# Expert sweep of a decoder block: the scatter-add into the output in whole rows of 4 KB in one chain, with six whole product tiles

## The chip, the cores and the metric

The kernel runs on the 8 cores of one Trainium2 chip. Each core has its own sequence of the batch (4096 tokens of 1024 values) and its own copy of all weights; the cores do not exchange data. The time is that of the slowest core in microseconds (us). A core has TensorE (PE: matmuls and transposes), VectorE (DVE), ScalarE (ACT), GpSimd (POOL: here it issues the indirect DMAs and writes their descriptors) and SyncE (SP: here it issues the weight loads), and 16 DMA engines that all queues share.

## The reference, cut to what matters

```python
h2 = modulate(rmsnorm(x, norm2_gain[l]), shift2, scale2)          # x: after the token mixer
# hierarchical_moe: top-1 group of 4, top-2 of its 4 experts; combine (T, 4, 4) has two nonzeros per token
for gi in range(N_EXPERT_GROUPS):
    a = jnp.einsum('td,edf->tef', hf, w_gate[gi])
    b = jnp.einsum('td,edf->tef', hf, w_up[gi])
    hid = jax.nn.silu(a) * b * combine[:, gi, :, None]
    out = out + jnp.einsum('tef,efd->td', hid, w_down[gi])
x = x + gate2[:, None, :] * y_moe
```

So each token goes through two of 16 experts, and two products of 1024 float32 values are added to its row of `x`.

## The kernel before

The first three quarters of the time are the token mixer, the router and the conversion of the expert weights to bfloat16 in DRAM (`w_bf`). They leave `x` in `out` (4096 rows of 4 KB and 128 spare rows) and the normalised tokens with their 16 weights in `h2d` (rows of 2112 bytes). The change touches only what follows, the function `moe` at the end: the sweep.

The sweep first computes on VectorE which token stands in which row of which block: 79 blocks of 128 rows, all rows of a block for one expert (`idx`, one column of 128 row numbers for each block; `idxh`, the same for rows of half the length). Then it goes through the blocks p = 0 to 78. Two lanes alternate: even p take blocks 0, 1, 2, ..., odd p take blocks 40, 41, .... Each lane has its own half of the six weight slots (`wts[p % 2]`), so an expert's weights stay while its blocks follow one another in the lane, and when the expert changes six chunks of 512 KB come anew. All instructions are in program order on each engine; the order of a step is in the loop at the end of `moe`:

- `gather(p + 6)`: POOL issues an indirect DMA that brings 128 rows of `h2d` into one of 7 buffers.
- `x_t(p + 2)`: PE transposes the block, ACT copies it out, DVE picks the weight of each row.
- `g_mm(p + 1)`, `u_mm(p + 1)`: 8 matmuls each for gate and up; ACT takes SiLU, DVE forms gate x up x weight.
- `d_t(p)`, `d_mm(p)`: PE transposes the hidden block and multiplies it with the down weights into PSUM banks 4 and 5, one bank for each half of the 1024 output columns.
- `scatter(b, 0)`, `scatter(b, 1)`, called in `d_mm`: DVE multiplies a bank by `g2b` (the gate) into a tile of 128 x 512 float32; POOL issues an indirect DMA that adds the 128 rows of 2 KB to the output (`compute_op=ALU.add`).
- `w_load(p + 2, (4, 5))`, `w_load(p + 3, (0, 1, 2, 3))`: SP issues the weight chunks; where the expert stays, the address lies out of bounds and the DMA moves nothing.

A token can stand in two blocks, and an add reads a row, adds and writes it. So adds to the same bytes must not be in flight together. The kernel sees to it with one region for each half of the columns, `r_outh[0]` and `r_outh[1]`: POOL waits before each add until the last add to the same half has landed. There are thus two chains, and an add of the left half and one of the right half may be in flight together. While POOL waits, all that stands behind in its order waits too, the gathers among it.

The product tiles are a ring of 11 halves (`yp`): six in the three `f32a` tiles, five in `BB`. DVE waits before it overwrites a tile until that tile's add has landed.

The trace names all operations that the helper `K.op` records as L166; the gathers are L1272, the adds L1358, the weight loads L1287. The product tiles show up as `f32a<-PS,g2b` and `BB<-PS,g2b`, the adds as `out<-f32a,BB` and `out<-BB`, the weight chunks as `slot<-w_bf`.

Of the kernel before, what the change touches and what calls it, by code (L numbers as in the profile page):

```python
# [6 lines left out]
F32 = mybir.dt.float32  # L7
BF16 = mybir.dt.bfloat16
F16 = mybir.dt.float16
I32 = mybir.dt.int32  # L10
U8 = mybir.dt.uint8
AF = mybir.ActivationFunctionType
ALU = mybir.AluOpType
# [8 lines left out]
NB = 79  # L22
# [196 lines left out]
def build_nc(n_st=4, dbg=False, upto=None):  # L219
# [36 lines left out]
    out = nc.dram_tensor("out", [T + 128, D], F32, kind="ExternalOutput").ap()  # L256
# [6 lines left out]
    K = Sync()  # L263
    es = ExitStack()

    def sb(name, shape, dt):
        return es.enter_context(nc.sbuf_tensor(name, list(shape), dt))
# [13 lines left out]
    g2b = sb("g2b", [128, 1024], BF16)  # L281
# [32 lines left out]
    f32a = RR([sb(f"f32a{i}", [128, 1024], F32) for i in range(3)], "f32a")  # L314
# [21 lines left out]
    bank_r = [Region(f"bank{i}") for i in range(8)]  # L336
# [17 lines left out]
    def bank(i, w=512, off=0):  # L354
        return PS[:, i * 512 + off: i * 512 + off + w]
# [101 lines left out]
    for g in range(8):  # L457
# [17 lines left out]
         reads=[r_c0], writes=[r_c])  # L475
    K.op("act", lambda e: e.activation(out=esink[:], in_=esink[:], func=AF.Exp), reads=[r_const], writes=[r_const])
    K.op("dve", lambda e: e.tensor_tensor(out=WmT[:], in0=wsf[:].rearrange("p (g t) -> p g t", g=8),
                                          in1=mkt[:, 0:128].unsqueeze(1).to_broadcast([128, 8, 128]), op=ALU.mult),
         reads=[wsf_r, mkt_r], writes=[r_const])
# [13 lines left out]
    for hh in range(2):  # L493
        K.op("pe", lambda e, hh=hh: e.matmul(PS[0:1, (b0 + hh) * 512:(b0 + hh + 1) * 512], ones_bf[:, 0:1],
                                            WmT[:, 4 * hh:4 * hh + 4, :], start=True, stop=True),
             reads=[r_const], writes=[br_[hh]])
    K.op("act", lambda e: e.activation(out=r2r[0:1, :], in_=PS[0:1, b0 * 512:(b0 + 2) * 512], func=AF.Copy),
         reads=br_, writes=[r2r_r])
    b0, br_ = nb(2)
    for g in range(8):  # L500
        K.op("pe", lambda e, g=g: e.matmul(PS[:, b0 * 512 + g * 128: b0 * 512 + (g + 1) * 128], r2l[0:2, g, :],
                                          r2r[0:2, g * 128:(g + 1) * 128], start=True, stop=True),
             reads=[r_const, r2l_r, r2r_r], writes=[br_[g // 4]], inc=(g % 4 == 3))
# [20 lines left out]
    def ada_rows(units, dst, dst_r):  # L524
        for n_, u in enumerate(units):
# [13 lines left out]
         reads=[r_const, r_mod], writes=[r_const])  # L539
# [607 lines left out]
    def moe():  # L1147
        olds = [r_B1, r_B2] + r_acc
        r_lh = r_lhs[0]
        BBf = BB[:]  # L1150
        BH = BBf[:, 0:64 * NB].bitcast(F16).rearrange("p (a b) -> p a b", a=64)
        r_bh = K.alias("bh", olds)
        o_ = 64 * NB
# [6 lines left out]
        idx = BBf[:, o_:o_ + 2 * 80].bitcast(I32)  # L1160
        tab = BBf[:, o_ + 160:o_ + 320].bitcast(I32)
        r_idx = K.alias("idx", olds)
        r_tab = K.alias("tab", olds)
        o_ += 320
        o_ += (-o_) % 16
        ys = [f32a.tiles[i][:, 512 * h:512 * (h + 1)] for i in range(3) for h in range(2)]
        ys_r = [K.alias(f"y{i}{h}", [f32a.regs[i]]) for i in range(3) for h in range(2)]
        for i in range(5):
            ys.append(BBf[:, o_ + 1024 * i:o_ + 1024 * (i + 1)].bitcast(F32))
            ys_r.append(K.alias(f"y{i}b", olds))  # L1170
        yp = RR(ys, "y")
        idxh = [BBf[:, 16064 + 160 * h:16224 + 160 * h].bitcast(I32) for h in range(2)]
        outh = out.rearrange("t (h c) -> (t h) c", h=2)
        r_outh = [K.alias(f"out{h}", [r_out]) for h in range(2)]
        NXG = 7
        hTf = hT[:].rearrange("p k t -> p (k t)")
        xgs = [hTf[:, 1056 * i:1056 * (i + 1)] for i in range(NXG)]
# [4 lines left out]
        def bid(p):  # L1182
            return p // 2 if p % 2 == 0 else LANE + p // 2
# [13 lines left out]
        W = [r_wk]  # L1197

        def wop(fn, reads=(), writes=None):
# [3 lines left out]
                                      in1=row[:, 148:179].unsqueeze(1).to_broadcast([128, 16, 31]), op=ALU.is_gt), reads=ptr_)  # L1203
# [7 lines left out]
        for sh in (1, 2, 4, 8):  # L1211
# [8 lines left out]
             reads=W + [r_oh], writes=[tmp_r])  # L1220
# [4 lines left out]
        for s_ in range(4):  # L1225
            K.op("dve", lambda e: e.tensor_tensor(
                out=BH[:, 16 * s_:16 * s_ + 16, :], in0=bk[:, 16 * s_:16 * s_ + 16].unsqueeze(2).to_broadcast([128, 16, NB]),
                in1=iob.unsqueeze(1).to_broadcast([128, 16, NB]), op=ALU.is_equal), reads=W + [r_const], writes=[r_bh])
            K.op("dve", lambda e: e.tensor_tensor(
                out=BH[:, 16 * s_:16 * s_ + 16, :].rearrange("p (k b) n -> p k b n", k=2),  # L1230
                in0=BH[:, 16 * s_:16 * s_ + 16, :].rearrange("p (k b) n -> p k b n", k=2),
                in1=col[:, 8 * s_:8 * s_ + 8].unsqueeze(1).unsqueeze(3).to_broadcast([128, 2, 8, NB]), op=ALU.mult),
                 reads=[r_bh, r_const], writes=[r_bh])
        pi, pir = nb(1)
        for a in range(64):
            K.op("pe", lambda e, a=a: e.matmul(bank(pi, NB), LH[:, a, :], BH[:, a, :], start=(a == 0), stop=(a == 63)),
                 reads=[r_lh, r_bh], writes=pir, inc=(a == 63))
        va = wk[:, 592:592 + NB]
# [3 lines left out]
        wop(lambda e: e.tensor_scalar(out=vb, in0=bank(pi, NB), scalar1=0.0, scalar2=col[:, 32:33], op0=ALU.is_equal, op1=ALU.mult), reads=pir)  # L1242
        wop(lambda e: e.scalar_tensor_tensor(out=va, in0=va, scalar=2048.0, in1=vb, op0=ALU.add, op1=ALU.add))
        K.op("dve", lambda e: e.tensor_copy(out=idx[:, 0:NB], in_=va), reads=W, writes=[r_idx])
        for h in range(2):
            K.op("dve", lambda e: e.tensor_scalar(out=idxh[h][:, 0:NB], in0=va, scalar1=2.0, scalar2=float(h), op0=ALU.mult, op1=ALU.add),
                 reads=W, writes=[r_idx])

        K.op("dve", lambda e: e.tensor_tensor(out=ehot, in0=iob.unsqueeze(2).to_broadcast([128, NB, 16]),
                                              in1=cumb.unsqueeze(1).to_broadcast([128, NB, 16]), op=ALU.is_ge),  # L1250
             reads=W + [r_const], writes=[r_eh])
# [4 lines left out]
                                              in1=eb.unsqueeze(2).to_broadcast([128, NB, 16]), op=ALU.is_equal),  # L1256
             reads=W + [r_const], writes=[r_eh])
# [85 lines left out]
        def d_mm(p, ht, ht_r):  # L1343
            for fl in range(4):
                for dh in range(2):
                    c_ = 4 + fl // 2
                    K.op("pe", lambda e, fl=fl, dh=dh, c_=c_: e.matmul(
                        bank(4 + dh), ht[:, fl * 128:(fl + 1) * 128],
                        wts[p % 2][c_][:, (fl % 2) * 1024 + dh * 512:(fl % 2) * 1024 + (dh + 1) * 512], start=(fl == 0), stop=(fl == 3)),
                         reads=[ht_r, wts_r[p % 2][c_]], writes=bank_r[4 + dh:5 + dh], inc=(dh == 1 and fl % 2 == 1) or fl == 3)  # L1350
            b = bid(p)
            for dh in range(2):
                scatter(b, dh, *yp.next())

        def scatter(b, dh, y, y_r):
            K.op("dve", lambda e: e.tensor_tensor(out=y, in0=bank(4 + dh), in1=g2b[:, 512 * dh:512 * (dh + 1)], op=ALU.mult),
                 reads=bank_r[4 + dh:5 + dh] + [r_g2], writes=[y_r])
            K.dma_call("pool", lambda e: e.indirect_dma_start(  # L1358
                out=outh, out_offset=bass.IndirectOffsetOnAxis(ap=idxh[dh][:, b:b + 1], axis=0),
                in_=y, in_offset=None, compute_op=ALU.add),  # L1360
                       reads=[r_idx, y_r], writes=[r_outh[dh]])

        ys_r[0:6] = [K.alias(f"y{i}{h}", [f32a.regs[i]]) for i in range(3) for h in range(2)]
        yp.regs = ys_r
        AHEAD = NXG - 1
        for p in range(AHEAD):
# [8 lines left out]
        for p in range(NB):  # L1375
            if p + AHEAD < NB:
                gather(p + AHEAD)
            if p + 2 < NB:
                x_t(p + 2)
            if p + 1 < NB:  # L1380
                sl = g_mm(p + 1)
            ht = d_t(p, *hd)
            if p + 1 < NB:
                hd = u_mm(p + 1, *sl)
            d_mm(p, *ht)
            if p + 2 < NB:
                w_load(p + 2, (4, 5))
            if p + 3 < NB:
                w_load(p + 3, (0, 1, 2, 3))

    try:
        for st_ in range(n_st):
            body(st_)
        conv_step(len(conv))
        moe()
    except _Stop:
        pass
# [88 lines left out]
```

How the kernel before makes its waits and increments, by code:

```python
            def body(eng):  # L156
                for item in self.prog[e]:
                    if item[0] == "wait":
                        eng.wait_ge(sems[item[1]], item[2])
                    elif item[0] == "call":
                        ins = item[1](eng)
                        if item[2] is not None:
                            ins.then_inc(sems[item[2]], item[3])
                    else:
                        name, a, k = item[1]
                        ins = getattr(eng, name)(*a, **k)
                        if item[2] is not None:
                            ins.then_inc(sems[item[2]], item[3])
```

## Time and profile before

| | us |
|---|---|
| median of 3 runs | 2673.39 (2668.78 to 2675.87) |
| the profiled execution | 2670.27 |
| its span on the slowest core (core 0) | 2668.6 |
| spans of the other cores | 2640.1 to 2662.5 |

The whole page has PE busy for 1933.4 us, DVE for 1105.5, ACT for 870.2 and POOL for 670.0; these are sums over stages with different limits. The sweep's blocks run from about 2065 us to the end at 2668.6. In the trace, the first product of the sweep is formed at 2081 us and the last at 2642 us.

How to read the views: times are in us from the first instruction. A row of the timeline has the start, the duration, the engine, the line, the operation and `out<-in`, and in brackets how long the engine had been idle before and what ended that. The DMA view gives for a stretch the packets and bytes of each queue and the share of the time of all 16 DMA engines that its packets took; q0 is POOL's queue (gathers and adds), q1 is SP's (weights, and before the sweep the plain loads and stores). From a share, the length of the stretch and 16 engines follows the engine time of a packet.

### The profile page before, as it was taken

The numbers are of one execution on the slowest core, as the hardware profiler recorded it, in microseconds if no ns is written. First come the engines' busy times: TensorE is split into PE (matmuls) and PEld (weight loads), VectorE is DVE, ScalarE is ACT, GpSimd is POOL, SyncE is SP. The second block draws the span as 40 slices with busy tenths as digits, with TensorE's granted clock in tenths as the row PEclk, the third lists the DMA queues.
The fourth block names the chain that finished last, engine by engine and source line by source line (L and its number), as shares of the span: only waits on it lengthen the run. The fifth ranks groups of instructions, "written<-read, shape, count | busy, mean of one in ns | idle before, by whom it ended". The sixth has DMA issues, their size and how long they took to land.

```text
span 2668.6 us, 37330 instructions; the slowest of 8 cores (2640.1 to 2668.6 us)
## 1 busy us (share of the span) xinstructions
PE 1933.4 (72%) x10857; PEld 986.8 (37%) x11023; DVE 1105.5 (41%) x2174; ACT 870.2 (33%) x1356; POOL 670.0 (25%) x658
## 2 busy tenths in 40 slices
PE   1557619966675798667579866758982889888895
PEld 1223314434333344423334442334452444444442
DVE  1354512345445425544543554453356223332332
ACT  0416511134155324315531441553130222222231
POOL 1200520011103301110430111042010455555564
PEclk9989559987896699789679978967995988899998
DMA  7763898864306946420693442062132898999987
GB/s 122 165 120 71 96 111 157 146 214 159 67 32 75 117 129 186 167 56 32 82 130 121 141 160 56 32 80 95 64 119 73 231 207 170 191 184 214 188 163 142
DMA packets 124569, 337.87 MB, mean 127 GB/s; under 512 B 26762, under 2 KB 56850, under 8 KB 114132
## 3 DMA queue, kind: packets, MB, share of 16 engines
q0 software_dynamic: 79264, 200.26, 45.1%
q1 hardware_dynamic: 45108, 135.21, 14.4%
q8 instruction: 95, 1.56, 0.3%
q14 instruction: 102, 0.84, 0.1%
HBM read 526.89 MB, written 136.32 MB: 249 GB/s over the span
## 4 chain that ended last, share of the span: by engine, by line
PE 50%; DVE 15%; DMA 14%; issue 9%; ACT 8%; POOL 2%; SPq 1%; DVEq 1%; ACTq 0%; POOLq 0%; another core or an unknown queue 0%
PE PS L166 50%; DMA slot<-w_bf 6%; ACT FH L166 4%; DVE PT L166 4%; DVE small L166 3%; DVE BB L166 3%; DVE f32a L166 2%; DMA slot<-w_ada 2%; ACT bfh L166 2%; DMA triu<-k_tri 1%; DVE hT L166 1%; DMA slot<-w_out 1%; POOL small L166 1%; ACT f32a L166 1%; DMA out<-f32a,BB 1%
## 5 line engine op out<-in xcount | busy, mean ns | idle before, releaser
L166 PE MATMUL PS<-hT,slot 128*128 128x512 bf16 x2256 | 535.0, 382 | 12.2 <-DMA slot<-w_in 8.1
L166 PE MATMUL PS<-slot,B 128*128 128x512 bf16 x1701 | 445.5, 404 | 94.1 <-DMA slot<-w_bf 70.9
L166 PEld LDWEIGHTS PS<-hT,slot 128*128 128x128 bf16 x2304 | 226.0, 99 | 272.5 <-issue 22.0
L166 PEld LDWEIGHTS PS<-slot,B 128*128 128x128 bf16 x1776 | 171.6, 103 | 292.1 <-issue 148.9
L166 ACT ACTIVATE bfh<-PS 128x512 bf16<-128x512 f32 (+2 forms) x431 | 233.4, 595 | 72.0 <-PE PS L166 70.7
L166 POOL TENSOR_TENSOR PT<-bfh,etab 128x512 bf16<-128x512 bf16 (+1 forms) x128 | 147.6, 1164 | 429.8 <-ACT bfh L166 310.4
L166 POOL TENSOR_TENSOR small<-small 128x1 f32<-128x1 f32 x96 | 78.2, 815 | 696.6 <-DVE small L166 696.6
L166 PE MATMUL PS<-BB,slot 128*128 128x512 bf16 x997 | 244.2, 385 | 1.9 <-issue 0.7
L166 ACT ACTIVATE FH<-PS,cst 128x512 f32<-128x512 f32 x128 | 88.0, 687 | 338.4 <-PE PS L166 338.3
L166 DVE SCALAR_TENSOR_TENSOR bfh<-PS,small,FH 128x512 bf16<-128x512 f32 x79 | 59.3, 751 | 320.6 <-PE PS L166 307.0
L166 ACT ACTIVATE B<-PS 128x1024 bf16<-128x1024 bf16 x79 | 80.9, 1024 | 333.0 <-PE PS L166 333.0
L166 PE MATMUL PS<-slot,hT 128*128 128x512 bf16 (+1 forms) x756 | 179.0, 402 | 2.2 <-issue 1.9
L166 DVE TENSOR_TENSOR PT<-bfh,etab 128x512 bf16<-128x512 bf16 (+1 forms) x128 | 130.6, 1020 | 113.4 <-ACT bfh L166 113.4
L1358 POOL DMA_INDIRECT out<-f32a,BB x88 | 137.5, 1563 | 138.9 <-DMA out<-f32a,BB 46.0
L166 ACT ACTIVATE FH<-PS 128x512 f32<-128x512 f32 x175 | 104.5, 597 | 170.8 <-PE PS L166 164.7
L166 PE MATMUL PS<-slot,bfh 128*128 128x512 bf16 x631 | 157.4, 394 | 1.2 <-DVE f32a L166 1.1
L166 PEld LDWEIGHTS PS<-BB,slot 128*128 128x128 bf16 x1024 | 101.4, 99 | 123.8 <-issue 6.4
L1358 POOL DMA_INDIRECT out<-BB x70 | 109.3, 1562 | 111.8 <-DMA out<-BB 41.8
L166 ACT ACTIVATE BB<-PS 128x512 bf16<-128x512 f32 (+1 forms) x96 | 71.0, 739 | 201.3 <-PE PS L166 200.7
L166 DVE TENSOR_TENSOR B<-PS,FH 128x512 bf16<-128x512 f32 x64 | 44.3, 691 | 188.8 <-ACT FH L166 188.8
L166 PE MATMUL PS<-vaug,PT 128*128 128x65 bf16 x1008 | 83.9, 235 | 52.3 <-DVE ytm L166 27.1
L166 PEld LDWEIGHTS PS<-slot,hT 128*128 128x128 bf16 x768 | 86.5, 114 | 87.1 <-issue 44.6
(157 smaller groups left out, 2276.5 us busy)
## 6 DMA issues: line engine op xcount, KB each, us to landing
slot<-w_bf SPq DMA_DIRECT2D x474, 512.0 KB
w_bf<-w_ch POOLq DMA_DIRECT2D x96, 512.0 KB
FH<-x SPq DMA_DIRECT2D x32, 512.0 KB
BB<-x SPq DMA_DIRECT2D x32, 512.0 KB
out<-BB SPq DMA_DIRECT2D x32, 512.0 KB
slot<-w_ada POOLq DMA_DIRECT2D x12, 1024.0 KB
slot<-w_in POOLq DMA_DIRECT2D x10, 1024.0 KB
h2d<-PT SPq DMA_DIRECT2D x32, 256.0 KB
```

What stands on the lines that cost most here:

```text
L166: ins = getattr(eng, name)(*a, **k)
L1358: K.dma_call("pool", lambda e: e.indirect_dma_start(out=outh, out_offset=bass.IndirectOffsetOnAxis(ap=idxh[dh][:, b:b + 1], axis=0), in_=y ...
```

## The change

Each block's product is now one tile of 128 x 1024 float32. DVE still fills it with two multiplies of 512 columns, and one indirect DMA adds its 128 rows of 4 KB to the output. The row numbers are those of `idx`, so the two operations that formed `idxh` are gone. There is one region for the output (`r_out`), so POOL waits before each add until the add before it has landed. The ring of product tiles has six whole tiles: the three `f32a` tiles and three in `BB`.

```diff
-        ys = [f32a.tiles[i][:, 512 * h:512 * (h + 1)] for i in range(3) for h in range(2)]
-        ys_r = [K.alias(f"y{i}{h}", [f32a.regs[i]]) for i in range(3) for h in range(2)]
-        for i in range(5):
-            ys.append(BBf[:, o_ + 1024 * i:o_ + 1024 * (i + 1)].bitcast(F32))
-            ys_r.append(K.alias(f"y{i}b", olds))
+        ys = [t[:] for t in f32a.tiles] + [BBf[:, o_ + 2048 * i:o_ + 2048 * (i + 1)].bitcast(F32) for i in range(3)]
+        ys_r = [K.alias(f"yb{i}", olds) for i in range(6)]
         yp = RR(ys, "y")
-        idxh = [BBf[:, 16064 + 160 * h:16224 + 160 * h].bitcast(I32) for h in range(2)]
-        outh = out.rearrange("t (h c) -> (t h) c", h=2)
-        r_outh = [K.alias(f"out{h}", [r_out]) for h in range(2)]
...
-        for h in range(2):
-            K.op("dve", lambda e: e.tensor_scalar(out=idxh[h][:, 0:NB], in0=va, scalar1=2.0, scalar2=float(h), op0=ALU.mult, op1=ALU.add),
-                 reads=W, writes=[r_idx])
...
             b = bid(p)
+            y, y_r = yp.next()
             for dh in range(2):
-                scatter(b, dh, *yp.next())
-
-        def scatter(b, dh, y, y_r):
-            K.op("dve", lambda e: e.tensor_tensor(out=y, in0=bank(4 + dh), in1=g2b[:, 512 * dh:512 * (dh + 1)], op=ALU.mult),
-                 reads=bank_r[4 + dh:5 + dh] + [r_g2], writes=[y_r])
+                K.op("dve", lambda e: e.tensor_tensor(out=y[:, 512 * dh:512 * (dh + 1)], in0=bank(4 + dh),
+                                                      in1=g2b[:, 512 * dh:512 * (dh + 1)], op=ALU.mult),
+                     reads=bank_r[4 + dh:5 + dh] + [r_g2], writes=[y_r])
             K.dma_call("pool", lambda e: e.indirect_dma_start(
-                out=outh, out_offset=bass.IndirectOffsetOnAxis(ap=idxh[dh][:, b:b + 1], axis=0),
+                out=out[:, :], out_offset=bass.IndirectOffsetOnAxis(ap=idx[:, b:b + 1], axis=0),
                 in_=y, in_offset=None, compute_op=ALU.add),
-                       reads=[r_idx, y_r], writes=[r_outh[dh]])
-
-        ys_r[0:6] = [K.alias(f"y{i}{h}", [f32a.regs[i]]) for i in range(3) for h in range(2)]
+                       reads=[r_idx, y_r], writes=[r_out])
+
+        ys_r[0:3] = f32a.regs
         yp.regs = ys_r
```

How the instructions stand on POOL near the end of the sweep, before: gathers (`hT<-h2d`) and adds (`out<-`), with the semaphores that POOL waits for ahead of each (`dve` is the product, `dpl` and a number an earlier DMA of POOL's queue).

```order
L1358 DMA out<-BB 8448x512 [waits dve,dpl6]
L1272 DMA hT<-h2d,BB 128x528 [waits pe]
L1358 DMA out<-BB 8448x512 [waits dpl11,dve,dpl8]
L1358 DMA out<-BB 8448x512 [waits dve,dpl9]
L1272 DMA hT<-h2d,BB 128x528 [waits pe]
L1358 DMA out<-f32a,BB 8448x512 [waits dpl14,dve,dpl11]
L1358 DMA out<-f32a,BB 8448x512 [waits dve,dpl12]
L1272 DMA hT<-h2d,BB 128x528 [waits pe]
```

The same stretch of POOL's order in the changed kernel.

```order
L1263 DMA hT<-h2d,BB 128x528 [waits dpl9,pe]
L1348 DMA out<-BB 4224x1024 [waits dve,dpl6]
L1263 DMA hT<-h2d,BB 128x528 [waits dpl11,pe]
L1348 DMA out<-BB 4224x1024 [waits dve,dpl8]
L1263 DMA hT<-h2d,BB 128x528 [waits dpl13,pe]
L1348 DMA out<-f32a,BB 4224x1024 [waits dve,dpl10]
```

Between two gathers there was a pair of adds, each with a wait for the add two before it; now there is one add, with a wait for the one just before it.

On VectorE, one step near the end of the sweep, before: the two multiplies that write the product are `BB<-PS,g2b`.

```order
L166 SCALAR_TENSOR_TENSOR bfh<-PS,small,FH 128x512 [waits pe,act]
L166 TENSOR_TENSOR BB<-PS,g2b 128x512 [waits pe,dpl8]
L166 TENSOR_TENSOR BB<-PS,g2b 128x512 [waits pe,dpl10]
L166 TENSOR_TENSOR bfh<-hT,BB 128x16 [waits dpl15]
L166 TENSOR_REDUCE small<-bfh 128x1 [waits dve]
```

And one step there in the changed kernel.

```order
L166 SCALAR_TENSOR_TENSOR bfh<-PS,small,FH 128x512 [waits pe,act]
L166 TENSOR_TENSOR BB<-PS,g2b 128x512 [waits pe,dpl2]
L166 TENSOR_TENSOR BB<-PS,g2b 128x512 [waits pe,dve]
L166 TENSOR_TENSOR bfh<-hT,BB 128x16 [waits dpl7]
L166 TENSOR_REDUCE small<-bfh 128x1 [waits dve]
```

The order is the same; the first multiply now waits for the add that frees the whole tile, and the second waits for the first.

## Rows read from the trace of the kernel before

**Rows 1.** Busy time of each engine, stretches inside the sweep and at its end.
```profile
core 0: us, PE busy (x) PEld busy (x) DVE busy (x) ACT busy (x) POOL busy (x), PEclk, DMA share, GB/s
2200.00:2300.00 100.00, 89.87 (x492) 43.46 (x500) 32.07 (x70) 28.46 (x40) 53.36 (x39) 0.89 0.86 168
2400.00:2500.00 100.00, 84.04 (x465) 40.83 (x473) 29.91 (x66) 27.43 (x39) 54.51 (x41) 0.91 0.94 201
2600.00:2668.00 68.00, 36.47 (x206) 17.70 (x208) 15.15 (x31) 12.01 (x18) 34.33 (x24) 0.84 0.75 143
```

**Rows 2.** Who waited for whom from 2000 us: total, times, longest.
```profile
PE PS L166 <- DMA slot<-w_bf: 70.9, 53, 4.3
```

**Rows 3.** Timeline of DVE: two steps whose weights are there.
```profile
2309.42 1.29 DVE L166 TENSOR_TENSOR BB<-PS,g2b 128x512 f32<-128x512 f32 x2 [0.76 <-PE PS L166]
...
2315.27 1.29 DVE L166 TENSOR_TENSOR BB<-PS,g2b 128x512 f32<-128x512 f32 x2 [0.76 <-PE PS L166]
```

**Rows 4.** All adds (L1358), and the idle time of POOL before them.
```profile
L1358 POOL DMA_INDIRECT out<-f32a,BB x88: 1550/1554/1640, 2082.9 to 2661.5; - x88
L1358 POOL DMA_INDIRECT out<-BB x70: 1550/1554/1579, 2104.7 to 2650.7; - x70
its engine sat idle before it (us, times) until:
  DMA out<-f32a,BB: 64.6, 26
  PE PS L166: 59.8, 50
  DMA out<-BB: 58.4, 24
  DVE small L166: 22.6, 8
  DVE bfh L166: 20.4, 13
  issue: 18.0, 32
  DVE BB L166: 4.1, 3
  DVE f32a L166: 3.0, 2
```

**Rows 5.** Timeline of DVE and POOL, the last product and the adds behind it.
```profile
2642.42 1.29 DVE L166 TENSOR_TENSOR f32a<-PS,g2b 128x512 f32<-128x512 f32 x2 [1.93 <-PE PS L166]
...
2653.82 1.55 POOL L1358 DMA_INDIRECT out<-f32a,BB  x1 [1.58 <-issue]
2656.27 1.55 POOL L1358 DMA_INDIRECT out<-f32a,BB  x1 [0.90 <-DMA out<-BB]
2659.21 1.55 POOL L1358 DMA_INDIRECT out<-f32a,BB  x1 [1.39 <-DMA out<-f32a,BB]
2661.45 1.55 POOL L1358 DMA_INDIRECT out<-f32a,BB  x1 [0.70 <-DMA out<-f32a,BB]
```

**Rows 6.** Chain that ended last: start, duration; one add from issue to landing.
```profile
2653.82 4.63 DMA out<-f32a,BB
```

**Rows 7.** DMA view, 2640 to 2660 us: only adds in flight.
```profile
q0 software_dynamic: 994, 1.83, 68.9%
```

**Rows 8.** DMA view, 1958.9 to 1962.8 us: one plain store, 128 rows of 2 KB.
```profile
DMA packets 145, 0.28 MB, mean 71 GB/s; under 512 B 16, under 2 KB 16, under 8 KB 144
...
q1 hardware_dynamic: 144, 0.26, 17.9%
```

**Rows 9.** DMA view, 1962.8 to 1966.8 us: one plain store, 128 rows of 4 KB.
```profile
q1 hardware_dynamic: 144, 0.52, 32.2%
```

**Rows 10.** DMA view, 2252 to 2277.4 us: weights, adds and gathers together.
```profile
q1 hardware_dynamic: 1452, 5.26, 61.7%
q0 software_dynamic: 897, 1.91, 37.9%
```

**Rows 11.** DMA view, 2065 to 2669 us: the whole sweep.
```profile
q0 software_dynamic: 28969, 62.42, 64.3%
q1 hardware_dynamic: 13824, 50.34, 23.8%
```

**Rows 12.** Groups by form, 2040 to 2064 us: the two `idxh` operations are among these.
```profile
L166 DVE TENSOR_SCALAR BB<-BB 128x79 int32<-128x79 f32 x2 | 0.4, 201 | 0.2
```

## The prediction

> **What bounds the kernel now.** I read the stretches of the busy-time view first. Inside the sweep [rows 1] PE is busy for 84 to 90% and the DMA engines for 86 to 94% of the time; in the last 68 us PE falls to 54%. POOL is near 54% and DVE near 32% and bound nothing by their work. So two resources are close to full, and the question is which wait ends last. Where the weights of a step are there, PE sets the pace: the same DVE multiply comes every 2315.27 - 2309.42 = 5.85 us [rows 3]. From the first add (2082.9, [rows 4]) to the last product (2642.42, [rows 5]) there are 78 such steps in 559.5 us; at 5.85 us they would take 456 us. The other 103 us are stalls, and the list of waits names them: PE waits for the weight chunks, 70.9 us in 53 direct waits [rows 2]. So in the body of the sweep PE and, where an expert changes, the landing of 3 MB of weights are the bound.
>
> At the end it is another one. After the last product, eight adds are still to be issued or to land, and the kernel ends 26 us later (2668.6 against 2642.4 [rows 5]). The adds lag there by some four blocks, so the two chains of adds are not far from being a bound over the whole sweep. POOL's idle time ahead of the adds says the same [rows 4]: 123.0 us in 50 of 158 adds ended with the landing of an earlier add (64.6 + 58.4), and 109.9 us with PE or DVE, that is, with the product (59.8 + 22.6 + 20.4 + 4.1 + 3.0). Less some 13 us before the first add, 97 us are slack of the adds.
>
> **What one add costs now.** In the tail an add to one half starts at 2653.82 and the next to the same half at 2659.21, a pitch of 5.39 us [rows 5]. 4.63 of them are issue to landing [rows 6], the rest is POOL's reaction, 0.76. Of the 4.63, POOL writes descriptors for 1.55 [rows 4]. How long do the packets hold the DMA engines? Where only adds move, 994 packets take 68.9% of 20 us of 16 engines [rows 7]: 0.222 us each. A transfer of 128 rows is 144 packets, 128 rows and 16 small ones (under 512 B) [rows 8]; so an add holds each engine for 9 x 0.222 = 2.00 us. The other 3.4 us of the pitch are fixed.
>
> **What one add of 4 KB rows costs.** The trace has no add with such rows. It has plain stores with both: 2 KB rows take 0.179 x 3.9 x 16 = 11.2 us of engine time [rows 8], 4 KB rows 0.322 x 4.0 x 16 = 20.6 us [rows 9]. So 2 KB more in each row cost (20.6 - 11.2) / 16 = 0.59 us an engine for one stream, with nothing fixed of note. A 2 KB plain store holds an engine for 0.70 us and a 2 KB add for 2.00, nearly three times as long: an add has to fetch the product, fetch the old row, and write.
> - Lower bound: the two fetches overlap and only one stream is paid, +0.59. Pitch 5.98 us.
> - Upper bound: everything doubles, 4.00 us instead of 2.00. Pitch 7.39 us.
> - I take two streams one after the other, +1.18, with what is left of an add packet (0.222 less 2 x 0.074) as a fixed part that longer rows don't pay twice. Each engine is then held for 3.18 us, and the pitch is 6.57 us. It stands between the ends, a little nearer the lower; [rows 10] lean the same way: with weights alternating, q0's packets take 0.379 x 25.4 x 16 / 897 = 0.172 us, less than when adds run alone, so part of the 0.222 is waiting and not bytes.
>
> The descriptor writing stays at 1.55 us, 128 rows as before.
>
> **The change, part by part.**
> - *One chain instead of two.* Before, both halves shared the fixed 3.4 us of a pitch; now one add must do the whole block, and a block needs 6.57 us of chain instead of 5.39: 1.18 x 79 = +93 us of chain over the sweep. That is above PE's 5.85, so with weights present the adds now fall behind by 0.7 us a block, and catch up only while PE waits for weights. The slack of 97 us can absorb it where it lies next to a backlog. I count three quarters of it as usable (PE's stalls come in bunches, and a chain that has caught up starves): 73 us. The net is 93 - 73 = +20 us. Where the backlog reaches six tiles, DVE's first multiply waits for a free tile; behind it in DVE's order stand the next block's row weights and gate product, and PE's next `d_mm` waits for the banks 4 and 5. That is how a late add gets to PE.
> - *Less DMA time.* The adds of a block hold each engine for 3.18 instead of 4.00 us, 0.82 x 79 = 65 us of the 604 in [rows 11]. Where weights land, q0 has 37.9% and q1 61.7% of the engines [rows 10]; with adds a fifth cheaper q0 would fall to some 32 to 33% and the weights gain 8%. On 103 us of stalls that is -8 us.
> - *Ring of tiles.* 12 halves instead of 11, no term. A tile is now held until its whole row has landed, which is in the pitch.
> - *POOL.* 79 adds fewer at 1.55 us. POOL is half idle, and the gathers are six steps ahead: nothing. The gathers stand behind a waiting add; they need 1.02 us of an interval in which POOL waits anyhow.
> - *DVE.* The two operations for `idxh`, 0.2 us each [rows 12], stood ahead of the first gather: -0.5 us with their gaps. The add now starts after the second multiply: +0.6 on the first add. Together 0.
>
> Sum: 20 - 8 = +12 us. The profiled execution took 2670.3, so 2682; the median of the runs is 3.1 us above it, hence **2685**.
>
> A check from the other side, the chain alone, never starved: first add at 2083.6, then 78 pitches of 6.57 (512 us), and where weights move each of the 8 packets of an add lets one weight packet of 0.173 us [rows 10] go first, 1.4 us an add. Weights hold the engines for 0.238 x 604 = 144 us [rows 11], at 61.7% that is 233 us of the time or 29 adds: 40 us. The last add needs 7.15 + 1.18 from issue to the end. Sum 2644: this is a floor, some 38 us under my sum, and those are the starvation that the first sum has as unusable slack.
>
> The Trainium skill (DMA: Bandwidth & Descriptors, Anatomy of one DMA) gives about 2.0 us fixed and bytes / 436e9 for a DMA of POOL's queue, and advises to coalesce. By that, 256 KB more would be an estimated 0.6 us, the lower bound above, and the change would win. The trace does not agree for adds of today: by the rule the bytes of one are 0.6 us, the engines are held for 2.00. The same page (Queues, rings and completion order) says that a DMA engine goes round its queues packet by packet; that bears on the fourth rival.
>
> **Rivals.**
> 1. *Faster: only one stream is paid.* For it: the 0.172 us under mixed load, and that plain packets pay only bytes. Against it: add packets take three times as long as plain ones. Pitch 5.98: +47 us, all within the slack. The adds hold an engine for 2.59 instead of 4.00 us a block, weights gain 14% of 103 us, -15, and the four blocks of lag at the end shrink by two, -8. Together -23: 2650.
> 2. *Slower: an add's time goes with its bytes, or the row is moved as two 2 KB packets after all*, so that the change doesn't do what it says on the DMA engines. For it: the adding unit may be what takes the time, and nothing in the trace speaks of its rate. Pitch 7.39: +158 us, 73 absorbed, +85; the chain alone gives 2083.6 + 78 x 7.39 + 40 + 9 = 2709, +40. Between them +62: 2735. It decides from a pitch of about 7.1 us on, the mean of PE's steps with its stalls (559.5 / 78 = 7.17).
> 3. *Slower: the weights.* An add packet keeps its turn for 3.18 / 9 = 0.35 us instead of 0.22 before a weight packet gets one. While a backlog keeps q0 full, weights get 0.173 / (0.173 + 0.353) = 33% instead of 44% of an engine. Against it: one chain leaves 3.4 us free in each pitch, in which the weights have the engines alone. If it wins, the -8 turns into +19: 2712.
>
> **How the numbers follow.** Forecast 0.40, range of its own 2665 to 2705; rival 1 0.33; rival 2 0.17; rival 3 0.10. A run of this kernel can be told from no change from 0.3% on, that is 8 us: below 2665.4 is faster, above 2681.4 slower. Faster: 0.30 of rival 1 and 0.02 of the forecast, 0.32. Same: 0.03 and 0.12, 0.15. Slower: 0.26 of the forecast and rivals 2 and 3, 0.53. For the range I leave out the lower part of rival 1 and what lies above rival 2's middle, about a tenth each: 2648 to 2740.
>
> **What the profile after would show.** 144 packets for each add, so some 17,700 in q0 over the sweep (79 x (144 + 80 for a gather)) instead of 28,969, with the same bytes; twice as many per add would be rival 2's second half. A pitch of adds in the tail of 6.57 (5.98: rival 1; 7.39: rival 2). POOL's idle time before adds ended mostly by `out`, hardly by PE or DVE. More than 26 us from the last product to the end, up to six adds of 6.6 us. If DVE waits for an add (`out`) at all, the backlog filled the ring. PE's wait for weights: 65 us if the relief is right, above 80 if rival 3 is. I am wrong if the adds are no longer late at the end, or if PE's stalls, not the adds, carry the difference.

## The result: 2.7% slower

| | before | after |
|---|---|---|
| median | 2674.63 us (4 runs, 2668.78 to 2677.97) | 2746.85 us (4 runs, 2742.71 to 2885.77) |
| profiled execution | 2670.27 us | 2748.19 us |
| its span, slowest core | 2668.6 us (core 0) | 2746.6 us (core 2) |

The ratio is 1.0267, with a 95% interval of 1.0241 to 1.0294. (It, the ratios below and times given for single runs leave out executions in which the four cores of one die ran at a visibly lower TensorE clock; the highest time of after is one; the medians are over all runs.) Predicted were 2685 and "slower": the sign was right, the size was not, since +72 us stand against +12. The part before the sweep is the same in both kernels, but its length differs between executions: the first gather on core 0 starts between 2047 and 2067 us in the traces of this case, at 2060.6 in that of before and 2067.2 in that of after. That difference between the two profiled executions is no effect of the change.

The list of waits of the changed kernel, core 2, from 2000 us: who waited for whom, total, times, longest. It answers to [rows 2].

```profile
POOL out L1348 <- PE PS L166: 190.6, 38, 14.5
POOL out L1348 <- DMA out<-f32a,BB: 115.4, 19, 9.0
PE PS L166 <- DMA hT<-h2d,BB: 112.0, 43, 7.9
POOL out L1348 <- DMA out<-BB: 109.9, 18, 10.4
...
PE PS L166 <- DMA slot<-w_bf: 21.6, 17, 3.7
```

PE's wait for weights is down from 70.9 to 21.6 us, and in its place stands a wait that was hardly there: 112.0 us for the gathered rows `hT<-h2d`. That looks like a problem with the gathers. The rows of the adds say otherwise. First all 79 of them (against [rows 4]), then the end of the timeline (against [rows 5]).

```profile
L1348 POOL DMA_INDIRECT out<-f32a,BB x40: 1549/1586/1640, 2093.2 to 2737.5; - x40
L1348 POOL DMA_INDIRECT out<-BB x39: 1549/1586/1604, 2120.5 to 2731.0; - x39
...
DMA to landing us min/median/max: 5.7/6.7/12.5
```

```profile
2711.99 1.49 DVE L166 TENSOR_TENSOR f32a<-PS,g2b 128x512 f32<-128x512 f32 x2 [1.78 <-PE PS L166]
2717.52 1.56 POOL L1348 DMA_INDIRECT out<-BB  x1 [5.09 <-DMA out<-f32a,BB]
2724.22 1.55 POOL L1348 DMA_INDIRECT out<-BB  x1 [5.13 <-DMA out<-BB]
2731.01 1.55 POOL L1348 DMA_INDIRECT out<-BB  x1 [5.25 <-DMA out<-BB]
2737.47 1.55 POOL L1348 DMA_INDIRECT out<-f32a,BB  x1 [4.90 <-DMA out<-BB]
```

A pitch is the time from the start of one add to the start of the next in its chain. In the tail it is (2737.47 - 2717.52) / 3 = 6.65 us. Over the whole sweep it is (2737.5 - 2093.2) / 78 = 8.26 us. PE's own pace was 5.85 a block [rows 3], and 7.17 with its stalls for weights. So the chain is slower than PE all the way.

The chain that ended last, about 2500 us: start, duration, what.

```profile
2514.15 9.39 DMA out<-f32a,BB
2523.58 0.54 issue
2524.33 9.85 DMA out<-f32a,BB
2534.22 0.54 issue
2534.97 7.88 DMA out<-BB
2542.90 0.54 issue
2543.65 5.99 DMA out<-BB
2549.68 0.54 issue
2550.43 6.34 DMA out<-BB
```

Each add starts 0.8 us after the one before has landed, and nothing else stands between. That holds for the whole sweep: on this core 75 of the 78 adds behind the first start within 0.9 us of that landing, and the other three within 2.1. The list of waits above seems to say something else, since it puts 190.6 us of POOL's waits down to PE. An add waits for its product and for the add before it, and the list can name only one of the two. The next two rows are such a case, an add from issue to landing and the add behind it.

```profile
2460.15 6.47 DMA out<-f32a,BB
```

```profile
2467.41 1.59 POOL L1348 DMA_INDIRECT out<-f32a,BB  x1 [4.37 <-PE PS L166]
```

The first lands at 2466.62 and the second starts at 2467.41, 0.8 us later like all the others, though PE is named. So a wait that the list puts down to PE or DVE may well be one for the chain.

From issue to landing an add takes about 6 us, but 8 to 10 in the stretch from 2514 to 2543. What moves when an add is slow: first the DMA view of the tail (2717.5 to 2724.2 us, one add alone), then of 2439 to 2449.3 us, in which the add issued at 2436.69 and a gather behind it are on their way and weights land.

```profile
q0 software_dynamic: 144, 0.52, 48.7%
```

```profile
q1 hardware_dynamic: 552, 2.02, 60.5%
q0 software_dynamic: 215, 0.78, 40.0%
```

Alone, the add is 144 packets (no splitting of the 4 KB rows) and holds an engine for 0.487 x 6.7 = 3.26 us; the prediction had 3.18. Beside weights, 552 weight packets pass while q0 moves 215 (of the 224 of this add and its gather), 2.6 for one, and this add takes 12.55 us to land.

### The profile page after: what moved, and what is told of

Same layout as the page of the kernel before. It is cut to its first block, busy times and chain, and to the rows that moved or that the text cites. A ratio compares the mean times of both kernels' runs of the same rounds, so it can differ in the third digit from the quotient of the medians.

```text
span 2746.6 us, 37261 instructions; the slowest of 8 cores (2717.4 to 2746.6 us)
## 1 busy us (share of the span) xinstructions
PE 1948.7 (71%) x11023; PEld 989.4 (36%) x11023; DVE 1119.3 (41%) x2172; ACT 870.2 (32%) x1356; POOL 546.6 (20%) x579
## 4 chain that ended last, share of the span: by engine, by line
PE 40%; DMA 24%; DVE 15%; issue 9%; ACT 8%; POOL 2%; DVEq 1%; SPq 0%; ACTq 0%; POOLq 0%; another core or an unknown queue 0%
PE PS L166 40%; DMA out<-BB 8%; DMA out<-f32a,BB 6%; ACT FH L166 4%; DVE PT L166 4%; DVE small L166 3%; DVE BB L166 3%; DMA slot<-w_bf 2%; DVE f32a L166 2%; ACT bfh L166 2%; DMA slot<-w_ada 2%; DMA hT<-h2d,BB 2%; DMA triu<-k_tri 1%; DVE hT L166 1%; DMA slot<-w_out 1%
## 5 line engine op out<-in xcount | busy, mean ns | idle before, releaser
L166 PE MATMUL PS<-hT,slot 128*128 128x512 bf16 x2304 | 543.0, 384 | 10.4 <-DMA slot<-w_in 9.8
L166 PE MATMUL PS<-slot,B 128*128 128x512 bf16 x1776 | 457.0, 407 | 38.2 <-DMA slot<-w_bf 21.6
L166 PEld LDWEIGHTS PS<-slot,B 128*128 128x128 bf16 x1776 | 177.1, 105 | 236.3 <-issue 92.7
L166 ACT ACTIVATE B<-PS 128x1024 bf16<-128x1024 bf16 x79 | 80.9, 1024 | 407.6 <-PE PS L166 407.6
L166 PE MATMUL PS<-ident_b,hT 128*128 128x128 bf16 x632 | 53.9, 235 | 113.3 <-DMA hT<-h2d,BB 112.0
L166 PE MATMUL PS<-WmT,BB 128*128 128x128 bf16 x256 | 30.1, 301 | 116.7 <-DVE BB L166 116.7
```

The lines of the kernel that those rows point to most:

```text
L166: ins = getattr(eng, name)(*a, **k)
```

## The experiments

Two theories for the first round. A: the one chain of adds is the bound, the late gathers are how it reaches PE. B: the gathers are the bound, because they stand behind waiting adds in POOL's order. A third, C, says that the bytes and packets of the adds matter, by what they do to the weights.

**whole_lead10.** More buffers for the gathers, so that they are issued 10 steps ahead (four buffers lie in the part of `BB` that is free by then).

```diff
-        NXG = 7
+        NXG = 11
-        xgs = [hTf[:, 1056 * i:1056 * (i + 1)] for i in range(NXG)]
+        xgs = [hTf[:, 1056 * i:1056 * (i + 1)] for i in range(7)] + [BBf[:, 1056 * i:1056 * (i + 1)] for i in range(NXG - 7)]
-        r_xg = [K.alias(f"xg{i}", [r_lh]) for i in range(NXG)]
+        r_xg = [K.alias(f"xg{i}", [r_lh] if i < 7 else [r_bh]) for i in range(NXG)]
```

> The changed kernel with 11 gather buffers instead of 7, so that a gather is issued 10 steps ahead instead of 6. Theory A (the chain of adds is the bound): in the changed kernel one add follows the other almost without a gap, 78 pitches of 8.26 us in the mean; PE's 112 us of waits for gathers are only the way in which the late chain holds it. Then nothing is gained: 2747 within 10 us, the waits for gathers fall below 30 us and as much appears as DVE waiting for a free product tile. Theory B (the gathers are the bound: they stand behind waiting adds in POOL's order): PE's waits for gathers go and take their time with them, 2747 less 60 to 100, so 2650 to 2690.

Measured: 2748.39 us, ratio to before 1.0252 (1.0219 to 1.0285). Nothing is gained. The waits of its slowest core, 3:

```profile
DVE BB L166 <- DMA out<-BB: 138.2, 25, 12.6
DVE f32a L166 <- DMA out<-f32a,BB: 134.8, 26, 10.8
```

PE's wait for gathers is down to 9.9 us, and DVE now waits 273 us for a free product tile instead. Theory B is out: take away one place where the backlog is held, and it is held at the next one.

**whole_two_lanes.** Whole rows, but one chain for the even and one for the odd steps. Padding rows of both lanes went to the same spare rows; the odd lane gets 128 spare rows of its own in `out` and `h2d`.

```diff
+        r_outl = [K.alias(f"out{i}", [r_out]) for i in range(2)]
...
-                       reads=[r_idx, y_r], writes=[r_out])
+                       reads=[r_idx, y_r], writes=[r_outl[p % 2]])
...
+        vc = wk[:, 928:928 + NB - LANE]
+        wop(lambda e: e.tensor_scalar(out=vc, in0=bank(pi, NB)[:, LANE:NB], scalar1=0.0, scalar2=128.0, op0=ALU.is_equal, op1=ALU.mult), reads=pir)
...
+        wop(lambda e: e.tensor_tensor(out=va[:, LANE:NB], in0=va[:, LANE:NB], in1=vc, op=ALU.add))
```

> The changed kernel with whole rows of 4 KB, but two chains: POOL waits before an add for the last add of the same lane (even or odd steps), not for the one before. The padding rows of the odd lane go to spare rows of their own; the result is the reference's as long as the two lanes don't reach rows of the same token in neighbouring steps, which holds for this routing. Theory A: the chain was the bound, two whole-row adds in flight hide the 3.4 us fixed part; 2640 to 2675, PE hardly waits for gathers, fewer than three blocks of lag at the end. Theory B says the same for another reason. Theory C (the bytes: 4 KB adds hold the DMA engines and slow the weights, or each other): no more than a third of the 72 us comes back, 2720 or above.

Measured: 2694.2 and 2691.7 us. About 55 of the 72 us come back. The list of waits has no add any more that waits for an add, and on cores 4 to 7 each add for which the last landing of its lane is known (30 to 41 of 77 a core) starts 2 us or more after that landing. So the single chain was the main cause, and theory C's "no more than a third" is out. But the time stays 13 us above the kernel before as timed beside it (2680), and above the 2675 that theory A allowed.

**whole_no_weights, half_no_weights.** Every lane keeps its first expert's weights; the same edit in the changed kernel and in the one before.

```diff
+        wop(lambda e: e.memset(fr, 16.0 * CHB))
+        wop(lambda e: e.memset(fr[:, LANE:LANE + 1], 0.0))
         wop(lambda e: e.tensor_tensor(out=fr, in0=fr, in1=eb, op=ALU.add))
```

> The changed kernel in which each lane keeps the first expert's weights it loaded, so that no weights move during the sweep (the products are those of the wrong experts). Theory A with the pitch of 7.1 to 7.3 us that the trace shows between weight loads: first add near 2092, 78 x 7.2 = 562, 8 for the last: 2662, PE still waits for gathers or tiles, since 7.2 is above its 5.85. Of the 85 us gained all is the time that weight packets add to the chain. If PE were the bound instead: 2092 + 456 + 10 = 2560.

> The kernel before (halves, two chains), with no weights moving during the sweep in the same way. Two chains need 5.4 to 5.7 us a block, below PE's 5.85: PE's pace decides, 2081 + 78 x 5.85 + 10 = 2550, some 110 us less than the changed kernel without weights. If halves were held back by the chains too, 2600 or more.

Measured: medians of 2661.87 us and 2574.91 us, ratios to before 0.9948 (0.9896 to 1.0000) and 0.9603 (0.9567 to 0.9639). The first meets its forecast. The second is 25 us above it. All adds of whole_no_weights, core 6, and of half_no_weights, core 1:

```profile
L1350 POOL DMA_INDIRECT out<-f32a,BB x40: 1550/1587/1640, 2091.2 to 2645.2; - x40
```

```profile
L1360 POOL DMA_INDIRECT out<-f32a,BB x88: 1549/1553/1639, 2091.5 to 2564.8; - x88
```

In half_no_weights a block takes (2564.8 - 2091.5) / 78 = 6.07 us of adds, not the 5.4 to 5.7 that were expected. That is above PE's 5.85: the adds fall behind, the last product stands at 2545.53, and the kernel ends 27 us after it instead of 10. The rest of the 25 us is a later start (2091.5 instead of 2081).

In whole_no_weights the pitch is (2645.2 - 2091.2) / 78 = 7.10 us. So the weights add 8.26 - 7.10 = 1.16 us to a pitch, 90 us over the sweep, and PE waits for gathers even without them (70.0 us).

**whole_no_weights_no_gathers.** As whole_no_weights, and the gathers stop after the seventh (`if p >= 7: return` at the head of `gather`).

> whole_no_weights with no gathers after the seventh either, so that in the steps only the adds use the DMA engines and POOL (the blocks then repeat the first seven). Theory A: the one chain is the bound with the pitch of the tail, 6.65 us, at every step: 2091 + 78 x 6.65 + 8 = 2618, 37 to 44 us less than whole_no_weights (2656 to 2663, pitch 7.10); those 0.45 us a step are then what the gathers add to an add. If the difference between tail and body is something else (the other cores' traffic, the late tiles), the time stays at 2650 or above.

Measured: 2667.73 and 2658.11 us. The expectation of theory A failed: the time stays. Core 0, all adds and POOL's idle time before them:

```profile
L1352 POOL DMA_INDIRECT out<-f32a,BB x40: 1552/1557/1640, 2073.2 to 2623.7; - x40
...
  DMA out<-BB: 197.4, 36
  DMA out<-f32a,BB: 187.6, 34
```

(2623.7 - 2073.2) / 78 = 7.06 us, with nothing but adds in the core's queues. So the gathers cost the chain nothing, and 7.06 is its pitch undisturbed by its own core. Why the tail of the changed kernel is 0.4 us shorter stays open. That other cores are done by then doesn't look like the reason: the last two adds are 6.4 to 6.8 us apart on each of the eight cores of after, also on the one with the shortest span (core 5, 2717.4 us against 2746.6).

**half_one_chain.** The kernel before, rows of 2 KB, one chain.

```diff
-        r_outh = [K.alias(f"out{h}", [r_out]) for h in range(2)]
+        r_outh = [K.alias("out", [r_out])] * 2
```

> The kernel before with its rows of 2 KB and its 11 tiles, but one chain for both halves, so that never two adds are in flight. Theory A: each block needs two pitches of 5.39 us in the tail, 10.8, and more under load by the same factor as whole rows (8.26 to 6.65, 1.24), 13.4: 2085 + 78 x 12 to 13.4 = 3020 to 3130. So going from two chains to one costs some 400 us, and whole rows give about 300 of them back. If the number of chains mattered little and the row size a lot: below 2800.

Measured: ratio 1.1497 (1.1473 to 1.1520), 3072.08 and 3074.99 us, as theory A expected. Going to one chain alone costs 400 us; whole rows give some 325 of them back. The 72 us of the change are the difference of these two large parts. Core 3:

```profile
L1358 POOL DMA_INDIRECT out<-f32a,BB x88: 1549/1552/1639, 2075.8 to 3051.7; - x88
```

Its 158 adds have a pitch of (3051.7 - 2075.8) / 157 = 6.2 us.

**whole_store.** The changed kernel with `compute_op=ALU.add` left out.

> The changed kernel with the same one chain of whole rows, but each DMA writes its rows instead of adding them (the output then lacks x and one of the two products). A plain store of 4 KB rows holds an engine for 1.29 us instead of 3.26. Theory A: issue to landing falls from 5.9 to some 4 us, the pitch to 4.8 us, below PE's 5.85; the chain is no bound any more and weights get more of the engines: 2610 to 2645. If the chain's fixed part under weight traffic (POOL's descriptors, the landing) were what counts and not the add's own work, 2700 or more would stay.

Measured: 2633.61 us, ratio 0.9830 (0.9792 to 0.9867), within theory A's range. Core 5:

```profile
L1348 POOL DMA_INDIRECT out<-f32a,BB x40: 961/984/1005, 2090.5 to 2623.4; - x40
...
DMA to landing us min/median/max: 3.3/3.5/10.1
```

The same chain with a landing of 3.5 us instead of 6.7 (medians) is no bound. So it is what an add takes beyond a store that makes one chain too slow: of the 3.2 us, 0.6 are POOL's descriptors (984 against 1586 ns), the rest lies behind them, in the read, add and write.

**half_four_lanes.** Before, with a chain for each half and lane: in `scatter` the region is `r_outh[dh + 2 * (p % 2)]`, and the spare rows are as in whole_two_lanes.

> The kernel before (rows of 2 KB), with four chains instead of two: POOL waits before an add for the last add of the same half and the same lane. Padding rows of the odd lane go to spare rows of their own, as in whole_two_lanes, so the two differ in the size of the rows alone. Theory A (chains bound the adds): no add waits for an add any more, the 26 us from the last product to the end shrink to some 12, and PE's stalls for weights stay near 70 us: 2655 to 2668, faster than both kernels. Theory C (with the chains out of the way the adds crowd the weights): PE's waits for weights rise above 80 us, as they did in whole_two_lanes (87), and the time is 2675 to 2695. Against whole_two_lanes: equal if rows of 4 KB cost the weights nothing extra; 20 to 30 us less if they do.

Measured: 2673.92 us, ratio 1.0000 (0.9988 to 1.0013). The list of waits has no add that waits for another (on core 6 the landing before is known for all 154 adds that have one in their chain, and none starts less than 3.7 us after it), and the slowest core ends 12 us after its last product:

```profile
2664.27 1.29 DVE L166 TENSOR_TENSOR f32a<-PS,g2b 128x512 f32<-128x512 f32 x2 [1.93 <-PE PS L166]
...
2668.82 1.55 POOL L1363 DMA_INDIRECT out<-f32a,BB  x1 [0.30 <-issue]
```

Half of the lag at the end is gone as expected, and nothing is won: PE's wait for weights, 63.4 us before in the mean of the eight cores, is 73.5 here. The time lies between the two theories' ranges (up to 2668 and from 2675) and so do the waits (near 70 and above 80). What was gained at the end was lost to the weights: adds that aren't held back take DMA engines that the weights need, as theory C has it, though by less than it said.

**whole_two_lanes_lead10.** whole_two_lanes and the buffers of whole_lead10 together.

> whole_two_lanes (rows of 4 KB, one chain for each lane) with 11 gather buffers, gathers issued 10 steps ahead. In whole_two_lanes PE waits 9 to 11 us for gathers, nearly all at the start, and 70 to 87 us for weights. If the weights are the bound there: no change, 2690 to 2700. If late gathers hid behind another name: 10 us or more faster.

Measured: 2687.39 us, ratio 1.0054 (1.0039 to 1.0069). whole_two_lanes was 13 us over before and this is 14 over it as timed beside each, so late gathers hid nothing there. Whole rows stay 0.5%, some 14 us, slower than half_four_lanes, which has the same lanes. Slowest core, 5:

```profile
PE PS L166 <- DMA slot<-w_bf: 90.7, 52, 5.4
```

In the mean of the cores PE waits 79.5 us for weights, against 73.5 with rows of 2 KB. The rest of the 14 us I can't place.

**half_tail_lanes.** If two chains serve the weights and cost only at the end, four chains belong at the end alone.

```diff
+            if p >= 68 and not r_outt:
+                r_outt.extend(K.alias(f"outt{h}", [r_outh[h % 2]]) for h in range(4))
+            r_o = r_outt[dh + 2 * (p % 2)] if p >= 68 else r_outh[dh]
...
-                       reads=[r_idx, y_r], writes=[r_outh[dh]])
+                       reads=[r_idx, y_r], writes=[r_o])
```

> The kernel before with its two chains up to step 67 and four chains (half and lane, as in half_four_lanes) from step 68 on, where few weights or none are left to load. The lag of the adds at the end (26 us from the last product to the end) should shrink to some 13 us, as it did in half_four_lanes, while the adds don't crowd the weights before. Theory A/C together (two chains throttle the adds to the weights' good, and cost only at the end): 10 to 14 us less than before, ratio 0.995 to 0.996. If the lag of the end is made good anyway, or the last weights still move then: within 3 us of before.

Measured: 2670.14 us, ratio 0.9974 (0.9951 to 0.9996). It is the fastest of the versions that compute the whole result, some 7 us ahead of before, where 10 to 14 were expected; core 3 ends 12 us after its last product. Like all versions with lanes it rests on the routing: both experts of a token are in one group, the lanes meet in a group only around block 40, and the even lane comes there at its end, the odd lane at its start. With nearly all tokens in one group it would not hold.

## Why the prediction was right and wrong

- *The price of one add: right.* Of the three prices of a 4 KB row, the one taken, two streams after one another, was met in the tail: 3.26 us an engine against 3.18, a pitch of 6.65 against 6.57. The plain stores of both sizes [rows 8, 9] were the right rows to work it out from. Rival 1 (pitch 5.98) and rival 2 (7.39, or rows moved as two packets) are refuted there: q0 has 17,696 packets from 2065 us on, 17,700 were forecast. That the two streams really follow one another is not shown by this, only that their sum fits.
- *The slack of 97 us: this step failed.* I took the idle time that POOL's list ends with PE or DVE [rows 4] as time in which the chains had nothing to do, and three quarters of it, 73 us, as usable. There was no such time. The rows of before on core 6 (cores 4 to 7 have most of the landings of adds in their traces), two adds of one half and, for the first of them, issue to landing:

```profile
2458.85 1.55 POOL L1358 DMA_INDIRECT out<-f32a,BB  x1 [0.95 <-PE PS L166]
...
2465.14 1.55 POOL L1358 DMA_INDIRECT out<-f32a,BB  x1 [1.45 <-PE PS L166]
```

```profile
DMA to landing us min/median/max: 5.5/5.5/5.5
```

  The first lands at 2464.35 and the second starts 0.8 us later, though the list names PE. On this core 147 adds have a known landing of the last add to their half; 130 of them start within 0.9 us of it, and all that the 147 wait beyond 0.8 us comes to 10 us (10 to 11 us on cores 4, 5 and 7 too, where 100 to 126 are known). Where chains are not the bound this looks different, as half_four_lanes shows. So both chains were already busy without a break, at 7.4 us a block on core 0 ((2661.5 - 2082.9) / 78, [rows 4]), not at the 5.39 of the idle tail. The time of either kernel is first add + 78 steps + last add: 2083 + 78 x 7.4 + 7 before, 2093 + 78 x 8.26 + 9 after. Without the slack the prediction's own terms give 93 - 8 = +85 us; measured are +72. I had the sum of the chain, as the "check from the other side", used it as a floor, and explained its distance from the other one by starvation. It was the sum to trust. whole_lead10 shows that no lead or buffer helps against it.

  The pitch of a block, from the first and the last add, in the mean of the eight cores:

| us a block | with weights | without weights |
|---|---|---|
| rows of 2 KB, two chains | 7.27 (before) | 6.03 (half_no_weights) |
| rows of 4 KB, one chain | 8.21 (after) | 7.11 (whole_no_weights) |
| difference x 78 | 73 | 84 |

  The prediction's +1.18 us a block was near both differences (0.94 and 1.08). What was wrong was to let a reserve absorb most of it.
- *The pitch under load: mis-sized.* This is the term that made the sum of the chain too low. I had 6.57 and 40 us for the weights, together 7.08 in the mean. Measured are 7.06 to 7.10 without weights (38 to 41 us more over the sweep), and 90 us for the weights instead of 40. I let one weight packet go ahead of each packet of an add; in the trace 2.6 pass for one. [rows 10], where the two chains run, have 1.6 for one, and could have warned me: one packet in turn is not what they show either.
- *The gathers, "nothing": wrong in words, not in time.* A waiting add did hold up the gathers until PE waited 112 us for them. It costs nothing of its own: with gathers issued earlier (whole_lead10) or left out (whole_no_weights_no_gathers) the time stays.
- *Less DMA time for the adds, -8 us: not seen.* q0's share fell from 64.3% to 50.2% of the sweep, and PE's wait for weights fell to 21.6 us, but only because PE was late by then. Where PE isn't late, whole rows make the wait longer (79.5 against 73.5 us). Rival 3 was right on that point, with 6 to 14 us instead of 27.
- *The four blocks of lag as a sign that the chains are nearly a bound: right, and stronger than I took it.* They were never idle. Freeing them takes some 14 us off the end, and PE loses about as much to the weights (half_four_lanes), so in before the chains and the weights bound together.
- *The sign "POOL's idle time ends with `out`, hardly with PE or DVE": it seems to have failed* (211 of the 442 us before the adds name PE or DVE) and had not, since nearly every one of these adds, too, starts 0.8 us after a landing.

The Trainium skill's rule (DMA: Bandwidth & Descriptors, Queues, rings and completion order) has a DMA engine go round its queues packet by packet. The 2.6 to one don't contradict it if a turn can hold several rows, or if a packet of an add isn't ready when its turn comes; these runs don't tell the two apart, and it stays open. (What the prediction calls the fourth rival there is its third.)

## What to carry to other kernels

When transfers must follow one another, work out first + count x pitch + last before anything else, with the pitch under the load of the body, not that of an idle tail. To see whether such a chain has a reserve, subtract each landing from the start of the next transfer. What ended a wait by the profile is inferred, and where a transfer waits for two things it can name the wrong one (74 us of waits for PE and DVE on core 6 before, about 10 us of true reserve). A wait that appears on a new engine or buffer may be the backlog of a chain elsewhere: more buffers only move it (112 us for gathers became 273 us for tiles at the same time). And transfers that are held back can be a favour to those on the critical path: setting them free took 14 us off the tail and put 10 us on the wait for weights.

## What the hardware showed that was not expected

- POOL needs 0.98 us for an indirect store of 128 rows and 1.55 to 1.59 for an indirect add of the same rows (medians of 79 each); a gather takes 0.99 to 1.02.
- An indirect add of 128 rows of 4 KB lands 5.9 us after its issue when alone (tail of after), an indirect store 3.5 us in the median (whole_store, beside weights).
- Under weight loads a single add in flight takes up to 12.5 us on core 2 of after, while its packets and those of the gather behind it take 40% of the engines.
- One chain of 2 KB adds has a pitch of 6.2 us over the whole sweep (half_one_chain, core 3), against 8.26 for adds twice as long.
- With nothing but adds in its core's queues the chain of 4 KB adds still has a pitch of 7.06 us over the sweep (whole_no_weights_no_gathers), against 6.65 in the tail of after. Why is not known.
